# Feed-forward's first product on six of eight weight tiles as seven half-size products of sums of quarters

## The reference, cut to what matters

```python
h = rms_norm(x, norm2_g[l])                                   # (1, 1024, 1024)
f = jnp.square(jax.nn.relu(jnp.einsum('bsd,df->bsf', h, w_ff1[l])))   # w_ff1: 1024 x 4096
x = x + jnp.einsum('bsf,fd->bsd', f, w_ff2[l])                # w_ff2: 4096 x 1024
```

## Time and profile before

| | |
|---|---|
| median of the runs | 2422.44 us |
| span of the profiled execution, first to last instruction | 2422.4 us |
| PE busy | 2333.4 us |
| DVE busy | 1497.8 us |
| ACT busy | 989.8 us |
| POOL busy | 200.9 us |

### The profile page before, as it was taken

How to read it: one execution, slowest core, us unless ns; L and a number is a source line. 1 busy time by engine, 2 the same in 40 slices (tenths; PEclk the granted TensorE clock), 3 DMA queues, 4 the chain that set the end, 5 groups by cost and what they waited for, 6 DMA issues and landing times.

```text
span 2422.4 us, 30366 instructions
## 1 busy us (share of the span) xinstructions
PE 2333.4 (96%) x12906; PEld 1249.1 (52%) x12906; DVE 1497.8 (62%) x1897; ACT 989.8 (41%) x1496; POOL 200.9 (8%) x254
## 2 busy tenths in 40 slices
PE   7999999999999999999999977899999999989999
PEld 5445444444444444445544456654444446777765
DVE  6898856644644455588742389865534416989962
ACT  6245344221212121433322488842323216888841
POOL 0001030000000000533301100012000000000000
PEclk9999999999999999999999999999999999999999
DMA  5011000201111102013111010020130200010021
GB/s 184 35 60 45 1 35 36 104 35 70 36 70 35 70 35 70 1 37 116 59 70 35 1 36 1 1 105 35 70 139 29 76 2 1 1 36 1 1 88 53
DMA packets 50487, 116.02 MB, mean 48 GB/s; under 512 B 2418, under 2 KB 8107, under 8 KB 49968
## 3 DMA queue, kind: packets, MB, share of 16 engines
q1 hardware_dynamic: 48616, 105.40, 12.3%
q10 hardware_dynamic: 1736, 8.68, 0.9%
HBM read 101.49 MB, written 12.58 MB: 47 GB/s over the span
## 4 chain that ended last, share of the span: by engine, by line
PE 81%; DVE 10%; ACT 7%; issue 1%; DMA 0%; SPq 0%; DVEq 0%; ACTq 0%
PE PS L72 78%; PE PS L75 4%; ACT RG L81 3%; DVE mx L110 2%; DVE RG L107 2%; DVE R L93 2%; ACT OV L84 2%; DVE R L101 1%; DVE RG L93 1%; DVE RG L101 1%; ACT R L81 1%; DVE oss L110 1%; ACT mx L81 0%; DVE scl L110 0%; DMA R<-in_x 0%
## 5 line engine op out<-in xcount | busy, mean ns | idle before, releaser
L72 PE MATMUL PS<-R,RG 128*128 128x512 f16 (+1 forms) x5472 | 1163.6, 374 | 8.4 <-DVE R L101 4.2
L72 PEld LDWEIGHTS PS<-R,RG 128*128 128x128 f16 (+1 forms) x5472 | 540.4, 103 | 625.8 <-issue 10.5
L72 PE MATMUL PS<-RG,R 128*128 128x512 f16 (+1 forms) x2904 | 631.3, 378 | 2.2 <-DVE R L101 1.7
L72 PEld LDWEIGHTS PS<-RG,R 128*128 128x128 f16 x2904 | 283.4, 98 | 330.5 <-issue 3.0
L81 ACT ACTIVATE R<-PS,scl 128x512 f32<-128x512 f32 (+1 forms) x176 | 116.2, 685 | 646.8 <-PE PS L72 520.8
L101 DVE SCALAR_TENSOR_TENSOR R<-PS,scl,R 128x512 f32<-128x512 f32 (+1 forms) x227 | 161.5, 744 | 184.2 <-PE PS L72 163.5
L101 DVE SCALAR_TENSOR_TENSOR RG<-RG,scl 128x4096 f16<-128x4096 f32 (+2 forms) x52 | 190.6, 3665 | 54.1 <-ACT RG L81 54.1
L107 DVE TENSOR_TENSOR_SCAN RG<-RG 128x127 f32<-128x127 f32 (+7 forms) x128 | 168.4, 1343 | 80.2 <-ACT RG L81 80.0
L72 PE MATMUL PS<-R,OV 128*128 128x64 f32 (+2 forms) x1456 | 195.7, 276 | 5.7 <-DVE R L93 5.4
L110 DVE TENSOR_REDUCE scl<-RG 128x1 f32<-128x4096 f32 (+2 forms) x43 | 155.6, 3619 | 65.3 <-DMA RG<-in_a_w_in 24.7
L81 ACT ACTIVATE RG<-RG,scl 128x4096 f16<-128x4096 f32 (+2 forms) x52 | 158.6, 3050 | 90.2 <-DVE scl L113 90.2
(11 more groups left out here) (128 smaller groups left out, 1522.3 us busy)
## 6 DMA issues: line engine op xcount, KB each, us to landing
RG<-in_w_ff SPq DMA_DIRECT2D x16, 2048.0 KB, 8.2
RG<-in_a_w_in SPq DMA_DIRECT2D x8, 2048.0 KB, 8.6
xspill<-R ACTq DMA_DIRECT2D x2, 4096.0 KB, 16.3
RG<-in_w_kv SPq DMA_DIRECT2D x4, 2048.0 KB, 8.1
RG<-in_b_w_in SPq DMA_DIRECT2D x4, 2048.0 KB, 8.1
RG<-in_w_in SPq DMA_DIRECT2D x3, 2048.0 KB, 8.3
R<-in_x SPq DMA_DIRECT2D x8, 512.0 KB, 8.3
RG<-in_w_out SPq DMA_DIRECT2D x2, 2048.0 KB, 7.9
```

The lines of the kernel that those rows point to most:

```text
L72: return self.engine.matmul(*a, **k) if self.engine else Nothing()
```

## The change

Tiles 9, 11, ..., 19 (`SEVEN`) are no longer multiplied as one matrix of 1024 x 512, but by Winograd's form of Strassen's scheme. Weights and tokens are each cut in four quarters (input features low and high, columns or tokens left and right), and seven products of quarters or of sums of quarters take the place of eight: `up_seven`, 7 products x 2 blocks of 128 columns x 12 matmuls.

- The four sums of tokens are made once, by GpSimd (`token_sum`, 16 instructions of 128x512), in place in `SQ3` and `SQ2n`; ScalarE and VectorE split them into halves (`sum_high`, `sum_low`).
- The four sums of weight quarters are made for each of the six tiles by GpSimd, two instructions of 128x512 each: `first_sum` ahead of the all-reduce of the tile's peak, `third_sum` behind it, `second_sums` after VectorE has made the first low halves. ScalarE and VectorE convert a tile in four pieces (`seven_high`, `seven_second`, `seven_low`): a sum of 1024, the tile of 4096, and later, at uses 7 and 8 of the down pass, two pieces of 1024.
- A tile now needs seven quarters for its halves, and takes the room of two slots; the `DOWN` tiles from 8 to 20 share the third.
- The results are put together: products 1, 6 and 7 add up in one bank, from which ScalarE copies each step to `FT` (`up_copy`), products 5 and 3 in another, and VectorE adds banks and copies (`up_sum`). The relu follows in `FT`, on two blocks at a time.
- The tables of `MEASURE`, `CONVERT` and `LOW` move, and `split_f` moves two to five products further back.
- The bound for such a tile's numbers is 2^12 instead of 2^14, and 2^8 instead of 2^9 for the normed tokens.

The diff, cut to its core:

```diff
+for _j, _m, _c in ((7, None, (6, 7)), (8, (7, 2), (7, 3)), (9, (7, 7), (8, 1)),
+                   *((_d, (_d - 2, 11), (_d - 1, 1)) for _d in range(10, 22, 2)),
+                   *((_u, (_u - 2, 8), (_u - 1, 1)) for _u in range(11, 23, 2)),
...
+SEVEN = range(9, 21, 2)
+SECOND, SECOND_LOW = {(_i - 1, 7): _i for _i in SEVEN}, {(_i - 1, 8): _i for _i in SEVEN}
...
+            def up_seven(c):
+                i = UP[c]
+                for p in (1, 2, 6, 5, 7, 4, 3):
+                    for m in range(2):
+                        key = ("up", c, p, m)
+                        if p in (1, 2, 5, 4):
+                            b = banks.take(key)
+                            e.wait_ge(*sig("weight").at(i))
+                            e.wait_ge(*banks.free(key))
+                        else:
+                            b = banks.ap(("up", c, 5 if p == 3 else 1, m))
+                        if p in (6, 7):
+                            e.wait_ge(*sig("up_copy").at(c, 1 if p == 6 else 6, m))
+                        if p == 3:
+                            e.wait_ge(*sig("up_sum").at(c, 5, m))
+                        if p in (5, 6, 7, 4):
+                            e.wait_ge(*sig("t_low").at({5: 1, 6: 2, 7: 3, 4: 4}[p]))
+                        for k in range(4):
+                            for ws, hs in ((0, 0), (0, 1), (1, 0)):
+                                mm = e.matmul(b, seven_w(p, ws)[:, k, 128 * m:128 * m + 128], seven_h(p, k, hs),
...
             def feed(i, use):
-                if (i, use) in LOW:
+                if (i, use) in LOW and LOW[i, use] in SEVEN:
+                    seven_low(LOW[i, use], 0)
+                    seven_low(LOW[i, use], "tile")
+                elif (i, use) in LOW:
                     convert_low(LOW[i, use])
+                if (i, use) in SECOND_LOW:
+                    seven_low(SECOND_LOW[i, use], 1)
+                    seven_low(SECOND_LOW[i, use], 2)
...
+            def seven_high(i):
+                e.wait_ge(*sig("w_factor").at(i))
+                e.wait_ge(*full.at(*last_product.get(before_slot(i), ())))
+                e.wait_ge(*sig("w_added").at(i, 0))
+                e.activation(seven_extra(0, 0), SUM, ACT.Copy, scale=w_col(i, 2)).then_inc(*sig("w_high").up(i, 0))
+                e.wait_ge(*sig("w_added").at(i, "tile"))
+                e.activation(seven_tile(0), w_raw(i), ACT.Copy, scale=w_col(i, 2)).then_inc(*sig("w_high").up(i, "tile"))
...
+            def third_sum(i):
+                e.wait_ge(*sig("w_peak").at(i))
+                e.wait_ge(*sig("w_added").at(i, 0))
...
+            def second_sums(i):
+                e.wait_ge(*sig("seven_low").at(i, 0))
...
+                e.wait_ge(*sig("seven_low").at(i, "tile"))
...
             def feed(i, use):
+                if (i, use) in MEASURE and MEASURE[i, use] in SEVEN:
+                    first_sum(MEASURE[i, use])
                 if (i, use) in MEASURE:
                     measure(MEASURE[i, use])
+                if (i, use) in MEASURE and MEASURE[i, use] in SEVEN:
+                    third_sum(MEASURE[i, use])
+                if (i, use) in SECOND:
+                    second_sums(SECOND[i, use])
...
+            token_sum(1)
+            token_sum(3)
+            token_sum(2)
             up(0)
+            token_sum(4)
             up(1)
```

More of the change, by code:

```diff
@@ L266, in tile_slot @@
         def tile_slot(i):
+            if i in range(8, 21, 2):
+                return 2
             return i % 3 if i < 40 else i - 40
@@ L1085, in low_half, with seven_low @@
                 return e.scalar_tensor_tensor(low, src, f, high, ALU.mult, ALU.subtract)
+            def seven_low(i, j):
+                e.wait_ge(*sig("w_high").at(i, j))
+                up = sig("weight").up(i) if j == 2 else sig("seven_low").up(i, j)
+                if j == "tile":
+                    low_half(seven_tile(0), seven_tile(1), w_raw(i), w_col(i, 2)).then_inc(*up)
+                else:
+                    src = quarter(w_raw(i), 1, 0) if j == 2 else SUM
+                    low_half(seven_extra(0, j), seven_extra(1, j), src, w_col(i, 2)).then_inc(*up)
             def factor(i):
@@ L1522, in up @@
                     feed(UP[c], z + 1)
+                    if c == 1 and z in (4, 5):
+                        sum_low((3, 1)[z - 4])
                     if z == 0:
@@ L2217, in up, with up_copy @@
                         total(7)
+                    if c == 1 and z in (3, 4):
+                        sum_high((3, 1)[z - 3])
+            def up_copy(c, p, m):
+                mi, n = {1: (m, 0), 6: (m, 1), 7: (2 + m, 0)}[p]
+                e.wait_ge(*full.at("up", c, p, m))
+                e.wait_ge(*sig("f_low").at(c - 1, 1))
+                up = banks.empty([("up", c, 1, m)], sig("up_copy"), c, p, m) if p == 7 else sig("up_copy").up(c, p, m)
+                e.copy(FT[:, mi, cols512(n)], banks.ap(("up", c, 1, m))).then_inc(*up)
@@ L2561, in total, with first_sum @@
                 across(w_col(i, 1), w_col(i, 0)).then_inc(*sig("w_top").up(i))
+            def first_sum(i):
+                e.wait_ge(*sig("raw").at(i))
+                if i == 9:
+                    e.wait_ge(*sig("bank_full").at("up", 0, 3, 1))
+                raw = w_raw(i)
+                for x in range(0, 4, 2):
+                    up = sig("w_added").up(i, 0) if x else sig("pool_step").up()
+                    e.tensor_tensor(SUM[:, x:x + 2, :], quarter(raw, 0, 1)[:, x:x + 2, :],
+                                    quarter(raw, 1, 1)[:, x:x + 2, :], ALU.add).then_inc(*up)
@@ new lines, in token_sum @@
+            def token_sum(j):
+                out, a, b = {1: (T1, T3, T1), 3: (T3, T2, T3), 2: (T2, T2, T1), 4: (T4, T4, T2)}[j]
+                if j == 2:
+                    e.wait_ge(*sig("t_added").at(1))
+                    e.wait_ge(*sig("t_added").at(3))
+                if j == 4:
+                    e.wait_ge(*sig("t_added").at(2))
+                if j == 3:
+                    e.wait_ge(*sig("t_added").at(1))
+                e.wait_ge(*sig("h_low").at("norm2", 1, 7))
+                for k in range(4):
+                    up = sig("t_added").up(j) if k == 3 else sig("pool_step").up()
+                    e.tensor_tensor(out[:, k, :], a[:, k, :], b[:, k, :], ALU.subtract).then_inc(*up)
@@ L2594, in up @@
             def up(c):
-                for z in range(8):
+                for z in range(8 if c < 2 else 14):
                     feed(UP[c], z + 1)
```

170 lines of the change are left out of this document (157 added, 13 removed), and 2 rows, old and new, of the table DOWN.

## The result

The changed kernel takes 2431.9 us (median of five runs, 2427.3 to 2434.1), the kernel before 2422.4 us (2420.0 to 2424.0): a ratio of 1.0033 with an interval of 1.0017 to 1.0049 (the quotient of the two medians is 1.0039). It is slower, though it has 144 matmuls less. How much slower the times alone don't tell well: on the two chips of the experiments the kernel before had medians of 2423.7 and 2426.9 us, and single runs of it reached 2432.7 and 2432.8. The profiled execution after took 2427.26 us with a span of 2425.5 us, the fastest of the five; that is why the two traces differ by less than the two medians.

The account below looks back on a forecast made before the run. TensorE, busy 96% of the span, was taken to bound the kernel. Waits of 34.6 and 7.5 us plus 1.6 for the clock, less 31.1, gave +12.6 on 2422.4: 2435.0 us, range 2417 to 2453, the forecast's own 2428 to 2443.

Parts of the forecast that it names:

- A: Second up pass: token sums behind an all-reduce delay tile 8's conversion; TensorE waits 8.3 us, plus 1.3 for tile 7.
- What it removes: Six up passes lose 24 matmuls each, 144 at 0.216 us: 31.1 us less on the path.
- The changes, 5.85 and 6.97 us: GpSimd switching from sums to all-reduces costs 5.85 us, back 6.97 us; free only if GpSimd is idle anyway.
- Rival 2: Changes cost nothing because GpSimd's code stays loaded: 2402.2 us, chance 0.07.
- The port: GpSimd sums and VectorE instructions with two SBUF operands exclude each other, in order of arrival, lengthening both.
- Rival 3: Changes cost but the port doesn't, quarter sums slip between: 2420.0 us, chance 0.16.
- B: First down pass: tile 9's first part is late, so TensorE's tenth product waits 12.1 us for a residual's bank.
- C: Rest of first down pass and start of first new up pass: waits of 4.4, 0.5, 5.0 and 3.0 us.
- the clock: Lowered clock slows matmuls after a stall; counted once, after the last stall: +1.6 us.
- D: Five later pairs: the next tile loads late, so its copy makes TensorE wait 1.5 us each, 7.5 together.
- rival 4: D's chain is 2.5 us longer, a second bank also late, 4.0 us per pair: 2450.0 us, chance 0.27.

Follow-up runs that it names:

- experiment 7: Changed kernel with all sums on VectorE, tables refitted: token sums spread, down tiles measured at use 14, second sums at use 5; 2397.5 us, ratio 0.989.
- Experiment 6: Changed kernel with all sums on VectorE and a one-column sum on GpSimd at each former place, so all changes between kinds of work remain; 2402.5 us.
- experiment 5: Changed kernel with all sums on GpSimd, but the stretch's all-reduces made on TensorE and tile 8 converted one product later; 2408.1 us, ratio 0.993.
- Experiment 4: Changed kernel with only the 16 token sums moved to VectorE, weight sums left on GpSimd; 2413.8 us, ratio 0.9944.
- Experiment 8: Changed kernel with GpSimd's chain for tiles 9 to 19 made 2.5 us longer, half the last quarter sum made three times; 2448.6 us, ratio 1.0091.

## Why the prediction came out as it did

The forecast was 2435.0 us, and 2431.9 came; the verdict slower was right, and the mechanism too. That the two numbers lie so close is partly luck: in the stretch, where the forecast has +12.6 us, the trace has +5.6, and the profiled run (2427.3) lies below the narrower range of 2428 to 2443. One of the signs failed as well: VectorE was to wait some 11 us for GpSimd's results in A, and waited 18.59 and 3.70. The later pairs took 78.2 us (759.79 to 837.95) for a forecast of 79. The waits that I had named, 8, 12, 4, 5 and 3 us, came as 7.7, 10.0, 2.5, 3.2 and 2.6, in this order and for what I had said.

- **What it removes: 31.1 us.** Right. In experiment 7 the stretch is 29.1 us shorter with 1.9 us more of waits.
- **The changes, 5.85 and 6.97 us.** Right: 5.7 to 6.3 toward an all-reduce, 6.8 to 7.5 toward sums, 85.5 us ahead of the weight sums in all. Rival 2 is refuted by them. Experiment 6 shows that they cost next to nothing where no long sums stand in the same chain; what of the loss in the changed kernel is theirs, and what the sums', is parted by no run, only by the estimate for chain A above (13.1 and 5.1 us). (The Trainium skill, GPSIMD Engine Reference, 2.1 Instruction dispatch, speaks of about 6 us at the first call of a freshly loaded kernel. Here a wait of that size stands at every change, and the way toward sums is the longer by 1 us.)
- **The port.** Right in kind. Rival 3, without it, is refuted by the traces: in A twelve sums take 19.68 us for 12 x 1.23 = 14.8, and tile 7's low half 5.48. In chain A that is 4.9 us for a forecast of 5.6 (4.4 + 1.2). No run has sums and changes on GpSimd without the port, so its share of the loss is known only by these rows; in experiment 5 it is what makes the wait of 3.5 us, by the estimate there.
- **A: +1.3 and 8.3 us.** +1.0 and 7.73. Experiment 4 takes it away and gains 20 us of stretch with all that hangs on it.
- **B: 12.1.** 9.98. The end of the wait came where I had it: 486.4 forecast, 484.00 measured, in a trace in which TensorE began the stretch 2.2 us earlier (396.68 for 398.86). It was the beginning that came later, since the 108 matmuls ahead of it ran 2.6 us over.
- **C: 4.4 + 0.5, 5.0, 3.0.** 2.48, 3.16, 2.60. Here too slow matmuls take the room of waits: in A to C the waits come to 27.0 us more than before (2.06 + 7.73 + 9.98 + 2.48 + 3.16 + 2.60 - 1.06), the slow matmuls to 8.2 (with the 0.16 us at the end of each row), together 35.2 where I had 34.6 + 1.6 for the clock. I had worked with the ends, which the other engines set, and they held.
- **D: 7.5 us. This is the term that was mis-sized: it measured 1.0.** The chain of a later pair, counted from the start of the down pass at 707.4 us, against my steps (timelines of VectorE and ScalarE):

```profile
737.52 1.29 DVE L101 SCALAR_TENSOR_TENSOR RG<-RG,scl 128x1024 f16<-128x1024 f32 x1 [2.34 <-ACT RG L81]
...
746.70 4.42 DVE L110 TENSOR_REDUCE scl<-RG 128x1 f32<-128x4096 f32 x1 [5.92 <-DMA RG<-in_w_ff]
751.04 4.03 DVE L101 SCALAR_TENSOR_TENSOR R<-PS,scl,R 128x512 f32<-128x512 f32 x6
```

```profile
755.55 3.71 ACT L81 ACTIVATE RG<-RG,scl 128x4096 f16<-128x4096 f32 x1 [18.07 <-DVE scl L113]
759.17 1.05 ACT L84 COPY R<-PS 128x512 f32<-128x512 f32 x2
```

Tile ready at 31.4 us (forecast 31.6), the next one landed at 39.3 (40.0), measured at 43.7 (44.4), residuals done at 47.7 (48.3), the copy at 52.3 (53.3), needed at 51.8. Half of the error is the load: I had taken 8.35 us from the earlier trace rows, and here it is 746.70 - 738.81 = 7.9. Each step was right to half a microsecond. But the term was the difference of two long sums, 53.3 and 51.8, taken five times, and an error of 1 us in the chain is then 5 us in the time. Experiment 8 moves the same chain the other way by 2.5 us and gets 9.6 us of waits. This is near the condition of rival 4, and its 2448.6 us are near that rival's 2450.0, but not by its account: only one pair has the wait for a second bank and comes near its 4.0 us (1.18 + 2.60). In the stretch experiment 8 has +20.1 us where the rival has +27.6, and 7 us behind the stretch bring the times together.

Of 31.1 us gained, 27.0 are lost to waits in one stretch of 130 us, 1.0 later, and 8.2 to slow matmuls, which leaves +5.1; three times 0.16 us for the later waits make it the +5.6 that the traces have in the stretch. The medians differ by 9.6 us. The rest cannot be placed: only one execution after was profiled, the one with the highest clock (0.991, the others 0.989 and 0.990).

## What to carry to other kernels

Before work goes to an idle engine, read what it costs to change between its kinds of work, and whether the results stand in series: GpSimd was busy for 13% of the span and still set the end, since all-reduce, change, sum, change, all-reduce is a chain of 16 us even with two sums in it (0.4 + 7.0 + 2.5 + 5.9 + 0.4). The same 64 sums on the busier engine, 38.5 us of work on VectorE at 62%, cost 4.3 us of new waits, and 1.8 with tables fitted to them. And a term that is a small difference of two long chains, repeated, deserves a wide range of its own.

## What the runs showed beyond that

The time of one and the same program scatters by more than the 9.6 us between the medians, 2418.5 to 2432.7 us for the kernel before on one chip, and a place of it is visible. Behind the stretch of the table, in the rest of the program, no kernel here changes anything, and yet that rest takes 1419.5 to 1428.1 us. About 1060 to 1200 us behind the stretch's end (2060 to 2200 us in the kernel before), in the second block, the granted clock differs from trace to trace. In each trace these are the two windows of 70 us that begin 1057.5 us behind the end of the stretch, so that they hold the same work:

| | clock in the two windows | from the end of the stretch to the end of the span |
|---|---|---|
| before | 0.93, 1.00 | 1419.9 |
| after | 0.98, 0.98 | 1419.6 |
| 4: token sums on VectorE | 0.93, 0.94 | 1423.9 |
| 7: tables for VectorE | 0.90, 0.97 | 1427.0 |
| 8: a longer chain | 0.91, 0.90 | 1426.5 |
| 5: all-reduces on TensorE | 0.91, 0.90 | 1428.1 |

The rest is longest where the clock was lowest, and TensorE is busy for only 63.8 to 65.5 of the 70 us in each window, with short waits between. What starts it is not shown. For changes of a few microseconds the stretch of the trace that holds the change says more than the time of the whole.

Also, the cost of a wait goes beyond the wait, but not always. After most of the longer waits (2.48 to 10.63 us) 1.5 to 2.9 us went to slow matmuls. But 48 matmuls took the full-pace 10.53 us after 2.60 us (ahead of 770.56 in experiment 8) and after 2.58 us (experiment 6, 499.72), and the 24 after 3.16 us in the changed kernel took 5.35, also full pace; the slow ones came there behind the next wait.
